# First row tiles in pairs that share a staging slot, the second set ahead of the fourth weight group

## What is computed

```python
mod = c @ w_ada[layer] + b_ada[layer]
sh1, sc1, gt1, sh2, sc2, gt2 = jnp.split(mod, N_MOD, axis=-1)
h = modulate(rmsnorm(x, g_mix[layer]), sh1, sc1)
proj = h @ w_in[layer]
...
y = jnp.concatenate([ya.astype(x.dtype), yr], axis=-1) @ w_out[layer]
x = x + gt1[:, None, :] * y
h2 = modulate(rmsnorm(x, g_ffn[layer]), sh2, sc2)
f = jnp.square(jax.nn.relu(h2 @ w1[layer])) @ w2[layer]
x = x + gt2[:, None, :] * f
return rmsnorm(x, g_final)
```

## Time and profile before

| | us |
|---|---|
| median of 3 runs | 1176.4 |
| lowest, highest | 1175.57, 1176.73 |
| the profiled execution: span | 1176.1 |
| TensorE busy | 1132.5 (96%) |
| VectorE busy | 795.4 (68%) |
| ScalarE busy | 492.5 (42%) |

### The profile page before, as it was taken

How to read it: one execution, slowest core, us unless ns; L and a number is a source line. 1 busy time by engine, 2 the same in 40 slices (tenths; PEclk the granted TensorE clock), 3 DMA queues, 4 the chain that set the end, 5 groups by cost and what they waited for, 6 DMA issues and landing times.

```text
span 1176.1 us, 15924 instructions
## 1 busy us (share of the span) xinstructions
PE 1132.5 (96%) x6339; PEld 957.8 (81%) x6339; DVE 795.4 (68%) x690; ACT 492.5 (42%) x517; POOL 21.1 (2%) x27
## 2 busy tenths in 40 slices
PE   3879999999999999999999999999999999999996
PEld 1769989788778878888888888888888888888885
DVE  2577889987878898866565566565566565565675
ACT  2424454555534445443333444333444333444451
POOL 2000010000000001000000000000000000000000
PEclk9999999999999998999999999999999999999999
DMA  9999989999997956766666676666676666665551
GB/s 351 368 348 397 381 319 339 338 403 390 357 404 269 322 182 223 252 222 229 235 230 185 188 222 228 235 228 186 187 220 229 238 224 187 187 196 180 180 177 72
DMA packets 156749, 303.10 MB, mean 258 GB/s; under 512 B 5425, under 2 KB 73633, under 8 KB 148129
## 3 DMA queue, kind: packets, MB, share of 16 engines
q1 hardware_dynamic: 155248, 298.08, 72.4%
q10 hardware_dynamic: 832, 2.93, 0.6%
q0 software_dynamic: 624, 1.48, 0.4%
HBM read 300.36 MB, written 2.10 MB: 257 GB/s over the span
## 4 chain that ended last, share of the span: by engine, by line
PE 91%; DVE 4%; DMA 3%; issue 1%; ACT 1%; ACTq 0%; SPq 0%; DVEq 0%
PE ps_job L924 20%; PE ps_job L963 14%; PE ps_job L964 14%; PE ps_job L965 14%; PE ps_job L927 10%; PE ps_job L939 3%; PE ps_job L940 3%; PE ps_job L941 3%; DMA stage<-in_w_ada 2%; PE ps L1030 1%; DVE acc L1247 1%; DVE w_lo L1323 1%; DMA cst<-in_consts 1%; PE ps_job L1211 1%; PE ps_job L1209 1%
## 5 line engine op out<-in xcount | busy, mean ns | idle before, releaser
L1323 DVE TENSOR_TENSOR w_lo<-stage,w_hi 128x2048 fp32r<-128x2048 f32 x164 | 375.8, 2292 | 218.5 <-ACT w_hi L518 218.3
L518 ACT ACTIVATE w_hi<-stage 128x2048 fp32r<-128x2048 f32 (+1 forms) x167 | 318.0, 1904 | 424.0 <-PE ps_job L965 231.4
L924 PE MATMUL ps_job<-act_hl,w_hi 128*128 128x512 f32 x1024 | 322.4, 396 | 1.5 <-DVE w_lo L1323 1.1
L927 PEld LDWEIGHTS ps_job<-act_hl,w_lo 128*128 128x128 f32 x1024 | 192.7, 188 | 45.0
L927 PE MATMUL ps_job<-act_hl,w_lo 128*128 128x256 f32 x1024 | 201.2, 278 | 0.0
L963 PE MATMUL ps_job<-w_hi,hid_hl 128*128 128x512 f32 x480 | 188.1, 392 | 0.0
L964 PE MATMUL ps_job<-w_lo,hid_hl 128*128 128x512 f32 x480 | 187.0, 390 | 0.0
L965 PE MATMUL ps_job<-w_hi,hid_hl 128*128 128x512 f32 x480 | 186.9, 389 | 0.0
L924 PEld LDWEIGHTS ps_job<-act_hl,w_hi 128*128 128x128 f32 x1024 | 156.1, 189 | 2.5 <-DVE w_lo L1323 1.3
L1247 DVE SCALAR_TENSOR_TENSOR acc<-stage,small,acc 128x2048 f32<-128x2048 f32 (+1 forms) x56 | 122.9, 2195 | 7.2 <-DMA stage<-in_w_ada 3.5
L963 PEld LDWEIGHTS ps_job<-w_hi,hid_hl 128*128 128x128 f32 x480 | 90.1, 188 | 19.2 <-issue 0.7
(11 more groups left out here) (223 smaller groups left out, 1127.1 us busy)
## 6 DMA issues: line engine op xcount, KB each, us to landing
stage<-in_w SPq DMA_DIRECT2D x128, 1024.0 KB, 5.3
stage<-in_w_ada SPq DMA_DIRECT2D x64, 1024.0 KB, 7.8
stage<-in_w_in SPq DMA_DIRECT2D x41, 1024.0 KB, 8.5
stage<-in_w_ada SPq DMA_DIRECT2D x32, 512.0 KB, 6.9
stage<-in_w_out SPq DMA_DIRECT2D x16, 1024.0 KB, 7.7
gate_rows<-in_w_ada SPq DMA_DIRECT2D x16, 1024.0 KB, 7.0
x_sb<-in_x ACTq DMA_DIRECT2D x1, 2048.0 KB, 13.5
out_y<-f_acc SPq DMA_DIRECT2D x3, 512.0 KB, 2.7
```

The source lines that it names most:

```text
L518: nc.scalar.activation(w_hi[:, ring, 0:width], stage[:, slot, 0:width], ACT.Copy).then_inc(hi_ready, 1)
L924: nc.tensor.matmul(ps_job[:, 2 * pair + e, :], w_hi[:, ring, ws], act_hl[:, kt, :], start=(kt == 0), stop=False)
L927: last = nc.tensor.matmul(ps_job[:, 2 * pair + e, T:2 * T], w_lo[:, ring, ws], act_hl[:, kt, 0:T], start=False, stop=(kt == KT - 1))
L1323: nc.vector.tensor_tensor(w_lo[:, ring, 0:width], stage[:, slot, 0:width], w_hi[:, ring, 0:width].bitcast(F32), ALU.subtract).then_inc(lo_ ...
```

## The change

Tiles 0 to 31 become 16 items ("pair"): the even tile goes to the first half of a slot, the odd one to the second, each by its own DMA with its own semaphore (`stage_full` and the new `odd_full`). So six slots hold twelve tiles. The slot of item i is now `slot_of(i)`, which keeps the slots of the last items as they were. A slot of a pair is free when TensorE has summed its even tile and VectorE its odd one. `PAIRS_BEFORE` gives the pairs of the second set ahead of groups 0 to 3: pair 8 ahead of group 1, pairs 9 and 10 ahead of group 2, pairs 11 to 15 ahead of group 3. TensorE's sums of even tiles, which stood between groups, stand now after step k = 1 and after step k = 3 of the group before. The jobs, the groups and their order are the same, as is all arithmetic but the order of some sums; `EARLY` is empty and changes nothing.

```diff
+PAIRS_BEFORE = (0, 1, 3, 8)
 def tiles_before(g):
-    second = min(KT, (0, 2, 6, 9)[g] if g < OPEN else KT)
...
-    return KT + second + min(KT, max(0, 16 * (g - OPEN) // 15)) + later
+    return min(KT, max(0, 16 * (g - G_SET) // (G_B - 1 - G_SET))) + later
-ITEMS = [("tile", n) for n in range(KT)]
+ITEMS = [("pair", m) for m in range(KT // 2)]
 for _g in range(G_MLP):
+    while sum(i[0] == "pair" for i in ITEMS) < KT // 2 + PAIRS_BEFORE[min(_g, G_SET - 1)]:
+        ITEMS.append(("pair", sum(i[0] == "pair" for i in ITEMS)))
...
+def slot_of(i):
+    return (i - len(ITEMS) + STAGES + 1) % SLOTS
...
-                if freed and freed[0] == "tile" and freed[1] in PE_TILES:
-                    sp.wait_ge(tile_summed, freed[1] // 2 + 1 + freed[1] // KT)
-                elif freed and freed[0] == "tile" and freed[1] < KT:
-                    sp.wait_ge(tile_added, freed[1] // 2 + 1)
+                if freed and freed[0] == "pair":
+                    sp.wait_ge(tile_summed, freed[1] + 1 + freed[1] // (KT // 2))
+                if freed and freed[0] == "pair" and freed[1] < KT // 2:
+                    sp.wait_ge(tile_added, freed[1] + 1)
                 elif freed:
                     sp.wait_ge(lo_ready, READY[i - SLOTS])
-                load_group(src, i % SLOTS, 0)
+                load_group(src, slot_of(i), 0)
+                if what == "pair":
+                    sp.dma_start(stage[:, slot_of(i), G // 2:G].rearrange("p (k n) -> p k n", k=2), odd_src).then_inc(odd_full[slot_of(i)], 16)
...
-            def sum_second(g):
-                for n in range(KT, 2 * KT):
-                    if n in PE_TILES and (ITEM_OF_GROUP[g - 1] if g else 0) < ITEM_OF_TILE[n] < ITEM_OF_GROUP[g]:
-                        sum_early(n)
+            def sum_second(g, nth):
+                if nth < PAIRS_BEFORE[g] - PAIRS_BEFORE[g - 1]:
+                    sum_early(KT + 2 * (PAIRS_BEFORE[g - 1] + nth))
...
-                    if sums_between:
+                    if g < G_SET - 1 and k % 2 == 1:
+                        for nth in range(1) if k == 1 else range(1, KT):
+                            sum_second(g + 1, nth)
+                    if g == G_SET - 1:
                         finish_second(k)
```

More of the change, by code:

```diff
@@ L46, with w_in_jobs @@
 HALF = KT // 2
[L49 to L53, removed]
+SET_K = 4
+EARLY = ()
+def w_in_jobs(second):
+    k0 = HALF if second else 0
+    early = [("wide", QR0 + TOK_COLS * n, 0, SET_K) for n in EARLY]
+    jobs = [] if second else early
+    jobs += [("feat", KV0, k0, HALF)] + [("wide", Q0 + TOK_COLS * n, k0, HALF) for n in range(2)]
+    if second:
+        jobs += [("tok", VR0 + TOK_COLS, 0, KT)]
+        jobs += [("wide", QR0 + TOK_COLS * n, SET_K, KT - SET_K) if n in EARLY else ("wide", QR0 + TOK_COLS * n, k0, HALF) for n in range(4)]
+    else:
+        jobs += [("wide", QR0 + TOK_COLS * n, k0, HALF) for n in range(4) if n not in EARLY]
     jobs += [("tok", GR0 + TOK_COLS * n, k0, HALF) for n in range(2)]
     return jobs + [("tok", VR0, k0, HALF)]
-JOBS = w_in_jobs(0, []) + w_in_jobs(HALF, [("tok", VR0 + TOK_COLS, 0, KT)])
+JOBS = w_in_jobs(False) + w_in_jobs(True)
 JOBS += [("out_attn", TOK_COLS * n, 0, HALF) for n in range(STRIPS)]
 JOBS += [("out_ret", TOK_COLS * n, HALF, HALF) for n in range(STRIPS)]
-J_B = len(w_in_jobs(0, []))
+J_B = len(w_in_jobs(False))
 J_BQ, J_BGR = J_B + 1, J_B + 8
@@ L66 @@
 J_MLP = J_OR + STRIPS
-OPEN = 4
-N_GROUPS = [2] + [nk // (8 if kind == "feat" else 4) for kind, _, _, nk in JOBS[1:]]
-GROUPS = [(j, q) for q in range(2) for j in range(OPEN)] + [(j, q) for j in range(OPEN, len(JOBS)) for q in range(N_GROUPS[j])]
+J_KV = len(EARLY)
+J_CLOSED = J_KV + 4
+N_GROUPS = [2 if j == J_KV else nk // (8 if kind == "feat" else 4) for j, (kind, _, _, nk) in enumerate(JOBS)]
+FIRST_SET = [(j, 0) for j in [J_KV, *range(J_KV), *range(J_KV + 1, J_CLOSED)]]
+GROUPS = FIRST_SET + [(j, 1) for j in range(J_KV, J_CLOSED)] + [(j, q) for j in range(J_CLOSED, len(JOBS)) for q in range(N_GROUPS[j])]
+G_SET = len(FIRST_SET)
 FIRST = [GROUPS.index((j, 0)) for j in range(len(JOBS))]
@@ L88 @@
 CHUNKS_BEFORE = [0, 2, 4, 8]
[L89 removed]
+OPENING = [0, G_SET, G_B]
 HEAD_COLS = 2 * FEAT_COLS
@@ L117, with odd_fills @@
 ITEM_OF_GROUP = [i for i, item in enumerate(ITEMS) if item[0] == "group"]
-ITEM_OF_TILE = [i for i, item in enumerate(ITEMS) if item[0] == "tile"]
+ITEM_OF_PAIR = [i for i, item in enumerate(ITEMS) if item[0] == "pair"]
+ITEM_OF_TILE = [ITEM_OF_PAIR[n // 2] for n in range(2 * KT)] + [i for i, item in enumerate(ITEMS) if item[0] == "tile"]
 ITEM_OF_ROW = [i for i, item in enumerate(ITEMS) if item[0] == "row"]
-PE_TILES = [n for n in range(2 * KT) if n % 2 == 0]
-READY = [sum(i >= KT and not (what == "tile" and n in PE_TILES) for i, (what, n) in enumerate(ITEMS[:last + 1])) for last in range(len(ITEMS))]
-FILLS = [sum(i % SLOTS == slot for i in range(len(ITEMS))) for slot in range(SLOTS)]
+def odd_fills(i):
+    return sum(item[0] == "pair" and slot_of(m) == slot_of(i) for m, item in enumerate(ITEMS[:i + 1]))
+def slot_of(i):
+    return (i - len(ITEMS) + STAGES + 1) % SLOTS
+READY = [sum(i >= KT // 2 for i in range(last + 1)) for last in range(len(ITEMS))]
+FILLS = [sum(slot_of(i) == slot for i in range(len(ITEMS))) for slot in range(SLOTS)]
 V_MIX, V_FFN, V_BETA, V_GRET, V_C = 0, 16, 32, 40, 48
@@ L224, in build @@
         stage_full = [sem(f"stage_full{n}") for n in range(SLOTS)]
+        odd_full = [sem(f"odd_full{n}") for n in range(SLOTS)]
         gate_rows_full = [sem(f"gate_rows_full{n}") for n in range(2)]
@@ L353, in _ @@
             for i, (what, n) in enumerate(ITEMS):
-                if what == "tile" and n < 3 * KT:
+                if what == "pair":
+                    k, (k0, nk) = 2 * n % KT, SEGMENTS[2 * n // KT]
+                    src, odd_src = (w_ada[0, r * P:(r + 1) * P, :].rearrange("p (v n) -> p v n", v=6)[:, 0:2, k0 * P:(k0 + nk) * P] for r in (k, k + 1))
+                elif what == "tile" and n < 3 * KT:
                     k, (k0, nk) = n % KT, SEGMENTS[n // KT]
@@ L1534, in _ @@
                 for i in range(ITEM_OF_GROUP[g - 1] + 1 if g else 0, ITEM_OF_GROUP[g]):
-                    if g and ITEMS[i][0] == "tile" and ITEMS[i][1] not in PE_TILES:
+                    if g and ITEMS[i][0] == "tile":
                         sum_tile(ITEMS[i][1])
+                    elif g and ITEMS[i][0] == "pair":
+                        sum_tile(2 * ITEMS[i][1] + 1)
                     elif g and ITEMS[i][1] % 2:
                         add_rows(ITEMS[i][1] // 2)
-                if g == OPEN:
+                if g == G_SET:
                     copy_quarters(1, ps_job[:, 3, :], 2 * P)
```

56 lines of the change are left out of this document (30 added, 26 removed).

## The result

| | before | changed |
|---|---|---|
| median | 1176.6 (1175.6 to 1177.1, 4 runs) | 1182.1 (1181.5 to 1183.0, 4 runs) |
| span of the profiled execution | 1176.1 | 1180.9 |
| its time | not given | 1182.95 |

The ratio is 1.0045, interval 1.0031 to 1.0059: slower by 5.5 us, where the forecast was 2.8 and the range ended at 1181.5. By the same rule the profiled execution of the kernel before took about 1177.7 to 1178.2 us (an estimate), a little more than its median. The forecast, which put the median 0.3 above the span, had compared two different executions; a difference of spans isn't touched by that.

What follows compares the result with a forecast made beforehand. TensorE is full from 85 us, so group 5's start sets the end; before it SyncE's queue is the limit. Terms +0.9 + 1.9 + 0 = +2.8 us on 1176.4 gave 1179.2 us, range 1175.0 to 1181.5.

Steps and rivals of the forecast that it cites:

- Group 3 behind tile 31: Rounding, split and 24 matmuls of group 3 now stand ahead of `sum_quarters`: 70.6 us against 69.7 before, +0.9.
- The new idle time: TensorE idle from 60.1 to 67.9 us, so group 3's first matmuls run at low clock: +1.9 us, bounds 0 and 2.8.
- The estimate of 0.8 us: Low clock on group 3's first matmuls, by the skill's throttled 1.67 us per burst: 0.8 us, the sum 1.1 lower.
- TensorE's sums inside the groups: Even-tile sums, 0.53 us each, none added, covered by the wait for group 3's data: cost 0.
- The fixed rest: From the start of `sum_quarters` to group 5's first matmul: 11.4 us, which the change does not shorten.
- group 5's low spell: Low clock at group 5's start after 2.7 us idle, costing 1.5 us; kept in the sum, might fall otherwise (bound -1.5).
- Both dips go: DMA rate dips at 33 to 36 and 60 to 70 us vanish, giving back 4.6 us of transfer.
- the landing at 33.9 + 22 x 1.35 = 63.6: Group 3 lands 22 half-megabyte units of 1.35 us after group 0's landing at 33.9: 63.6 us.
- Crowding of x: Six more tiles in the queue may delay x, whose diagonal has 2.1 us slack: 0, 1 us kept for the range.
- The queue never runs dry between 20 us and group 4: SyncE's queue: groups 2 and 3 and pairs 11 to 15 can be issued at least 5 us ahead of their turn.
- Rival 4: Slower by more: the queue's pace falls to 1.45 us a unit, group 3 lands 2.2 us later: 1181.4; chance 0.12.

Runs made afterwards that it cites:

- the kernel kept warm: The changed kernel plus 56 matmuls whose result nobody reads, ahead of group 3 while TensorE waits for its weights; measured 1180.97 us, ratio 1.0026.

## Why the prediction was wrong

Right in direction and in what the new order costs; wrong in what the fuller queue gives back, and so too small by 2.3 us at `sum_quarters`. By its steps:

- **"Group 3 behind tile 31"**, as an order of work: confirmed. Rounding and split took 70.05 - 65.76 = 4.29 us (4.2 put), and the kernel with group 3 in its old place has `sum_quarters` at 66.34.
- **"The new idle time", +1.9:** confirmed. Steps 0 and 1 took 4.74 us; 2.8 + 1.9 was put. Keeping TensorE busy gave back 1.7. In the other kernels that waited so, the two steps took 4.7 to 5.4 us, so the change's spell is among the shorter. The estimate of 0.8 us from the figure of the Trainium skill ("TensorE: Matmul & The Clock Gate", "HAM oscillation") would have been too low.
- **"TensorE's sums inside the groups", 0:** confirmed (0.05 us).
- **"The fixed rest", 11.4 us, and group 5's low spell kept:** confirmed in this execution (86.19 - 74.79 = 11.40). Of the twelve kernels of the experiments only one has the spell in its profile (group 0 in rows of 2 KB), though nine of them have the same 2.7 us of idle time, so this was luck more than reading.
- **The step that failed: "Both dips go. This gives back 1.2 + 3.4 = 4.6 us"**, and with it the landing at 33.9 + 22 x 1.35 = 63.6. Both dips of the rate went, but only the second gave time back. At the first the queue was short too, but that was not what made the landings late: a fetch of TensorE's instructions had put one of the 16 parts of every transfer 1.5 us behind, with a short queue and with a full one. Filling the queue filled the dip with bytes of later tiles and moved no landing; with the pairs and the old order group 1 was rounded at 40.63, before at 40.75. The earlier trace rows held the warning: group 0 to group 1 was 6.84 us for four units, 1.71 each, where I took the pace from the six units behind. Put: 63.6. Measured: 65.76, so 2.2 us late. 1.5 of it is this place, 0.6 the first set.
- **Crowding of x, "0":** tile 15 came 0.6 us later in this execution, within the scatter of the others, and `x` came later in no other kernel with ten tiles in flight than with six. Nothing speaks against the 0.
- **"The queue never runs dry between 20 us and group 4":** held. Behind group 4 it does, at 77 to 83 us, which the forecast did not see and which cost nothing that is seen.
- **Rival 4** gave almost this time (1181.4) by a slower pace of the queue. That was not it: behind group 1 every unit took 1.35 us up to group 3.

The rest of the gap to the median, 5.5 against the span's 4.8, is of the size of the scatter between runs.

## What to carry to other kernels

A dip of the DMA rate is worth time only if the late issue there is also what ends last. Check it against the landings: units times pace from one landing to the next, at the very place of the dip. And when a refilled queue gives transfer time back, spend it on the wait that ends last: here the pairs alone gained 3 us, and the reordering that came with them put 4.3 us of rounding and split and 4.7 of matmuls at low clock between the last landing and the chain that sets the end.

## What the runs showed of the hardware

- A fetch of TensorE's instructions is a 16-KB packet that takes 1.1 us of one DMA engine. One of the 16 parts of every transfer behind it is then about 1.5 us late, up to the end of the burst. The landings are late by anything from nothing to all of it, according to how late that part had been before, while the total rate stays at 386 GB/s. The Trainium skill ("Runtime: NRT & Kernel Launch", "Instruction fetch mechanics") has the cost of crossing such a block as mostly hidden. Of the packets here that was so for some (33.3 with 72 extra matmuls: nothing); the one at 34.4 in the change cost 1.5 us.
- An extra matmul on plain float32 operands is four instructions of TensorE: 72 of them added 288 to the profile's count. The 56 of the kernel kept warm, on the operands in the rounded format, added 112, two each.
- SyncE can stand at an issue although the slot is free. In the change the tenth tile's issue took 7.9 us, where those of the first few took 0.5; no slot was used twice yet:

```profile
6.11 0.80 SPq L377 DMA_DIRECT2D stage<-in_w_ada  x1
6.95 7.88 SPq L401 DMA_DIRECT2D stage<-in_w_ada  x1
14.87 1.39 SPq L377 DMA_DIRECT2D stage<-in_w_ada  x1
```

- So slots for twelve tiles did not put twelve tiles in flight: of the nine issued ahead of that one, two had landed (4.9 and 6.4 us) when it began. That cost nothing that is seen here.
- TensorE's clock fell to 1.2 GHz in an idle stretch of 7.5 us, and 24 matmuls then took 4.74 us in place of 3.05. The other low spell, at group 5 after 2.7 us of idle time, came in three profiles (before, the change, group 0 in rows of 2 KB) and in none of the other eleven. It can't be forecast from the idle time ahead of it alone.
